# One core, two networks in a row: the RW lanes of the mixer stage split into an edge thread and a body thread

## The reference, cut to what matters

```
zr = z_rw + (token_shift(z_rw) - z_rw) * rw_mu
r, kr, vr, xw, xa, xg = split(zr)                       # 16 heads of 64
decay = exp(-exp(-softplus(-(rw_w0 + tanh(xw) @ rw_w2)) - 0.5))
a  = sigmoid(rw_a0 + xa @ rw_a2);  g = sigmoid(xg) @ rw_g2
kk = kr * rw_kk;  kk = kk / max(norm(kk), 1e-12)
kr = kr * (1 + (a - 1) * rw_ka)
S_t = S_{t-1} (diag(w_t) - kk_t^T (a_t*kk_t)) + v_t^T k_t ;  y_t = S_t r_t     # per head, 64 x 64
y  = groupnorm(y) * rw_ln_g + rw_ln_b + sum(r*kr*rw_rk) * vr;   y = y * g
out = concat([o_gla, y]) @ w_out
```

## Time and profile before

| | us |
|---|---|
| median of 3 runs | 3964.98 (3961.74 to 3965.10) |
| the profiled execution | 3966.74 |
| its span (first to last instruction) | 3965.0 |
| TensorE busy | 3651.3 (92%) |
| VectorE busy | 2321.6 (59%) |
| ScalarE busy | 1791.0 (45%) |
| mean granted TensorE clock | 0.946 |

### The profile page before, as it was taken

The page is one execution under the profiler, slowest core; times in us unless marked ns, Lnnn a source line. Parts: engine busy times, 40 slices in busy tenths (PEclk is TensorE's granted clock), DMA queues, the critical chain, the costliest instruction groups (busy, mean ns, idle before and its releaser), DMA issues.

```text
span 3965.0 us, 77817 instructions
## 1 busy us (share of the span) xinstructions
PE 3651.3 (92%) x29460; PEld 3538.5 (89%) x29460; DVE 2321.6 (59%) x3394; ACT 1791.0 (45%) x2463; POOL 217.2 (5%) x306
## 2 busy tenths in 40 slices
PE   7976989999999898888878899999998999999998
PEld 6976989999999898777767899999997999999998
DVE  3687566656665634454444566656656756856555
ACT  3322455544444533333333455544444546475443
POOL 1371100000000000000000200000000000000000
PEclk9988999999999998788888899999999999999999
DMA  4533556566656543111111466666664665556774
GB/s 132 152 112 96 152 145 181 170 177 189 175 167 176 160 128 91 43 43 38 43 38 49 123 184 182 177 198 183 181 175 130 165 167 146 152 138 177 196 193 143
DMA packets 1103441, 561.56 MB, mean 142 GB/s; under 512 B 23011, under 2 KB 1101429, under 8 KB 1102981
## 3 DMA queue, kind: packets, MB, share of 16 engines
q1 hardware_dynamic: 1100672, 553.98, 49.7%
q10 hardware_dynamic: 1957, 2.83, 0.2%
q0 software_dynamic: 624, 2.13, 0.2%
HBM read 556.77 MB, written 2.10 MB: 141 GB/s over the span
## 4 chain that ended last, share of the span: by engine, by line
issue 90%; POOLq 5%; PE 3%; DVE 1%; ACTq 0%; POOL 0%; ACT 0%; DMA 0%; DVEq 0%
POOLq L727 2%; POOLq L725 2%; POOLq L507 1%; PE ps L346 1%; PE ps L347 1%; PE ps L348 1%; PE ps L521 0%; ACTq L2130 0%; DVE arena L552 0%; POOLq L723 0%; PE ps L2154 0%; POOLq L2301 0%; DVE ps L548 0%; POOLq L2304 0%; POOLq L2224 0%
## 5 line engine op out<-in xcount | busy, mean ns | idle before, releaser
L314 DVE TENSOR_TENSOR w_lo<-raw,w_hi 128x1024 fp32r<-128x1024 f32 (+1 forms) x1136 | 1333.1, 1185 | 882.0 <-ACT w_hi L308 876.7
L308 ACT ACTIVATE w_hi<-raw 128x1024 fp32r<-128x1024 f32 (+1 forms) x1136 | 1144.0, 1016 | 696.5 <-PE ps L348 445.2
L346 PE MATMUL ps<-x_hi,w_hi 128*128 128x272 f32 (+1 forms) x3712 | 1076.7, 290 | 79.7 <-DVE w_lo L314 44.0
L347 PE MATMUL ps<-x_lo,w_hi 128*128 128x272 f32 (+1 forms) x3712 | 1072.4, 289 | 0.0
L348 PE MATMUL ps<-x_hi,w_lo 128*128 128x272 f32 (+1 forms) x3712 | 1072.0, 289 | 0.0
L430 PE MATMUL ps<-x_hi,w_hi 128*128 128x256 f32 (+4 forms) x2944 | 890.1, 302 | 56.3 <-DVE x_lo L546 16.2
L431 PE MATMUL ps<-x_lo,w_hi 128*128 128x256 f32 (+4 forms) x2944 | 849.0, 288 | 0.0
L432 PE MATMUL ps<-x_hi,w_lo 128*128 128x256 f32 (+4 forms) x2944 | 847.8, 288 | 0.0
L346 PEld LDWEIGHTS ps<-x_hi,w_hi 128*128 128x128 f32 x3712 | 715.7, 193 | 86.8 <-DVE w_lo L314 48.3
L347 PEld LDWEIGHTS ps<-x_lo,w_hi 128*128 128x128 f32 x3712 | 716.0, 193 | 0.0
L348 PEld LDWEIGHTS ps<-x_hi,w_lo 128*128 128x128 f32 x3712 | 715.3, 193 | 0.0
(11 more groups left out here) (442 smaller groups left out, 3396.5 us busy)
## 6 DMA issues: line engine op xcount, KB each, us to landing
raw<-ffn_w_up SPq DMA_DIRECT2D x352, 512.0 KB, 4.7
raw<-w_in SPq DMA_DIRECT2D x232, 512.0 KB, 3.8
raw<-cd_w_in SPq DMA_DIRECT2D x100, 512.0 KB, 3.8
raw<-ffn_w_down SPq DMA_DIRECT2D x128, 384.0 KB, 3.4
raw<-ab_w_in SPq DMA_DIRECT2D x80, 512.0 KB, 4.5
raw<-ffn_w_down SPq DMA_DIRECT2D x128, 320.0 KB, 3.3
raw<-w_out SPq DMA_DIRECT2D x48, 512.0 KB, 4.0
raw<-ab_w_out SPq DMA_DIRECT2D x32, 512.0 KB, 4.0
```

The source lines that it names most:

```text
L308: nc.scalar.activation(w_hi[:, j % SLOTS, 0:kt], raw[:, j % RING, 0:kt], ACT.Copy).then_inc(rounded, 1)
L314: nc.vector.tensor_tensor(w_lo[:, j % SLOTS, 0:kt], raw[:, j % RING, 0:kt], w_hi[:, j % SLOTS, 0:kt].bitcast(F32), ALU.subtract).then_inc( ...
L346: nc.tensor.matmul(acc, w_hi[:, j % SLOTS, k, 0:w], mh, start=first, stop=False)
L347: nc.tensor.matmul(acc, w_hi[:, j % SLOTS, k, 0:w], ml, start=False, stop=False)
```

## The change

The work of a lane is cut in two threads per engine, with semaphores of their own. `edge_*` does the front of a pair and its 16 meta tokens, in the lane's banks B + 1 and B + 2. `body_*` does the two tiles of 128 tokens (in all three banks), the chunk states and the end (in bank B alone). So the edge of a lane's next pair is issued beside the last states and the end of the pair before. Its gates wait for `fe2` of that pair, no longer for its end; its first wide tile waits for both the edge's `fe0` and the old pair's end.

```
+    def rw_start(p):
+        return MID_PARTS["pairs"] + 6 * p + 4.1
...
+    EDGE_AT, EDGE_END = timed((("keys", 1.0), ("gates", 1.9), ("rates", 2.0), ("norm", 0.6), ("cum", 3.4), ("decays", 0.1), ("bonus", 2.5), ("ready", 2.9),
...
+            ("x", 1.6), ("m", 1.5), ("p2", 1.0), ("p2_", 0.9), ("p4", 1.9), ("p4_", 1.1), ("p8", 1.3), ("p8_", 0.7), ("y8", 0.5), ("y8_", 0.7),
+            ("z1", 0.8), ("z1_", 0.7), ("w", 0.5), ("t32", 0.7), ("gh", 0.5), ("gh_", 0.6), ("fe", 2.6), ("fe_", 2.7))], BODY_END)
```

Four of the seven chunk states move into the second tile's steps. A state product is put behind the products of p4, p8, y8 and w, its addition behind theirs; only s6, s7 and s8 stay in a row:

```
+                mm = heads_times(B + 2, 0, L.p4, of(L.y), n, n)
+                if tt == 2:
+                    mm = next_state(2, B + 2, 2 * P)
+                done(mm)
...
+                mm = nc.vector.tensor_tensor(L.y, L.y, two_of(B + 2, 0, n), add)
+                if tt == 2:
+                    mm = next_state(2, B + 2, 2 * P)
+                done(mm)
```

Within a step, the mask that p2 needs (`q1`) is taken straight from PSUM ahead of the others, and p2 waits for it alone; `y` is waited for one step later. One ScalarE copy of 512 columns takes the place of two or three of 256 and 128 at p2 and p4:

```
-                done(nc.vector.tensor_tensor(L.p1[0:n, :, 0:n], res(2), over(low16), mult))
+                done(nc.vector.tensor_tensor(L.q1, ps[:, B:B + 2, 0:n], over(up16, n), mult))
...
-                vector(f"m{tt}")
+                vector(f"q1{tt}")
...
+                done(nc.scalar.activation(L.pq2, ps[:, B + 2].rearrange("p (a b) -> p a b", a=4), ACT.Copy))
```

```
+            for hh in range(2):
+                rows = slice(64 * hh, 64 * hh + 64)
+                if hh:
+                    pe.wait_ge(L.row_sem, 4 * q + 4)
+                for c in range(1, 9):
+                    state = L.state0[q % 2] if c == 1 else L.state[:, c - 1]
+                    first = P + (c - 1) * RW_CHUNK
+                    mm = nc.tensor.matmul(ps[rows, B, first:first + RW_CHUNK], state[rows], L.f[rows, c - 1], start=True, stop=True)
```

More of the change, by code:

```diff
@@ L204, in build @@
     low21, _ = place("low21", [P, P])
-    eye2, _ = place("eye2", [P, RW_N])
     seg, _ = place("seg", [P, T])
@@ L990, in build @@
     rws_s, RWS_S = sem("rws_scalar"), order("low")
-    def tile_stages(*stages):
-        return [f"{st}{tt}" for tt in range(3) for st in stages if tt or st not in ("z1", "w", "t32", "t16")]
-    RW_V = order("keys", "norm", "cum", "bonus", "ready", *tile_stages("p1", "m", "q2", "q4", "y4", "y8", "z1", "t32", "fe"),
-                 *[f"s{c}" for c in range(2, 9)], "y", "centred", "end")
-    RW_S = order("rates", "norm", "decays", *tile_stages("tok", "p2", "p4", "p8", "t16", "gh", "add"), "squared", "rstd")
@@ L1009, in build, with body_stages @@
-    RW_AT = {name: RW_LEN * x / at_ for name, x in RW_AT.items()}
-    def rw_start(p):
-        return MID_PARTS["pairs"] + 6 * (p + 1) + 0.1
-    def rw_vector(dve, lane_n):
-        L, mult, add, sub = lanes[lane_n], ALU.mult, ALU.add, ALU.subtract
-        B = L.b
-        yield GLA_END + 5.5
-        dve.drain()
-        nc.vector.memset(L.trans, 0.0)
-        dve.drain()
+    BODY_TILES = (1, 2)
+    def body_stages(*stages):
+        return [f"{st}{tt}" for tt in BODY_TILES for st in stages]
@@ new lines, in build @@
+    EDGE_V = order("keys", "norm", "cum", "bonus", "ready", "q10", "y0", "q40", "y40", "y80", "fe0")
+    EDGE_S = order("rates", "norm", "decays", "tok0", "p20", "p40", "p80", "gin0", "gh0", "add0")
+    EDGE_T = order("gates", "bonus", "x0", "p20", "p40", "p80", "y80", "gh0", "fe0")
+    BODY_V = order(*body_stages("p1", "q1", "y", "q4", "y4", "y8", "z1", "t32", "fe"), "s6", "s7", "s8", "y", "centred", "end")
+    BODY_S = order(*body_stages("tok", "p2", "p4", "p8", "gin", "t16", "gh", "add"), "squared", "log", "rstd")
@@ new lines, in build, with timed @@
+    BODY_T = order(*body_stages("x", "p2", "p4", "p8", "y8", "z1", "w", "gh", "fe"), "s6", "s7", "s8", "out", "sums", "squares", "gate")
+    RW_LEN = 2 * 6
+    def timed(stages, first=0.0):
+        at, now = {}, first
+        for name, step in stages:
+            at[name] = now
+            now += step
+        return at, now
+    EDGE_AT, EDGE_END = timed((("keys", 1.0), ("gates", 1.9), ("rates", 2.0), ("norm", 0.6), ("cum", 3.4), ("decays", 0.1), ("bonus", 2.5), ("ready", 2.9),
+                               ("x0", 1.3), ("m0", 1.1), ("p20", 0.3), ("p20_", 0.6), ("p40", 0.8), ("p40_", 0.7), ("p80", 0.5), ("p80_", 0.6),
+                               ("y80", 0.2), ("y80_", 0.5), ("gh0", 0.4), ("gh0_", 0.6), ("fe0", 0.5), ("fe0_", 1.2)))
@@ new lines, in build, with over, two_of, edge_vector @@
+    BODY_AT.update(some)
+    EDGE_AT, BODY_AT = ({name: RW_LEN * x / BODY_END for name, x in at_.items()} for at_ in (EDGE_AT, BODY_AT))
+    TAIL_AT = RW_LEN * TAIL_END / BODY_END
+    def rw_start(p):
+        return MID_PARTS["pairs"] + 6 * p + 4.1
+    def over(mask, n):
+        return mask[0:n, 0:n].unsqueeze(1).to_broadcast([n, 2, n])
+    def two_of(b, first, n):
+        return ps[0:n, b, first:first + 2 * n].rearrange("p (a b) -> p a b", a=2)
+    def edge_vector(dve, lane_n):
+        L, mult, add, sub, n = lanes[lane_n], ALU.mult, ALU.add, ALU.subtract, META
+        X, Y = L.b + 1, L.b + 2
@@ new lines, in edge_tensor, with body_tensor, of, value @@
+            done(mm)
+    def body_tensor(pe, lane_n):
+        L, n = lanes[lane_n], P
+        B = L.b
+        for q in range(PAIRS_RW // 2):
+            p = 2 * q + lane_n
+            done = lambda ins: ins.then_inc(L.bt, 1)
+            vector = lambda name: pe.wait_ge(L.bv, q * len(BODY_V) + BODY_V[name])
+            scalar = lambda name: pe.wait_ge(L.bs, q * len(BODY_S) + BODY_S[name])
+            at = lambda name: rw_start(p) + BODY_AT[name]
+            def of(buf, first=0):
+                return lambda hh: buf[:, first + hh]
+            def value(hh):
+                return L.v_tok[:, 64 * hh:64 * hh + 64]
+            def next_state(c, b, first):
+                before = L.state0[q % 2] if c == 1 else L.state[:, c - 1]
+                return nc.tensor.matmul(ps[:, b, first:first + RW_N], L.trans[:, c - 1], before, start=True, stop=True)
+            for tt in BODY_TILES:
+                t0 = TILES[tt][0]
+                cols_ = slice(t0, t0 + n)
```

584 lines of the change are left out of this document (342 added, 242 removed).

## The result

The changed kernel takes 3843.89 us (median of 4 runs, 3824.6 to 3850.05) where the kernel before takes 3965.04 us beside it: ratio 0.9676, 95% interval 0.9637 to 0.9715. The forecast was 3920 us in a range of 3870 to 3990 us. The direction is right; the gain is 121 us where 45 were forecast.

The account below looks back on a forecast made before the run. TensorE bounds the kernel, losing time to waits and low clock in the RW pairs. Waits -3.6, work -0.7 and clock -1.8 make -6.1 us a pair, -49 over eight, +4 at the end: 3920 us, range 3870 to 3990.

Parts of the forecast that it names:

- Waits that come: TensorE's waits per pair in the new order: 11.7 us, 10.5 as the trace counts, against 14.1 before; term -3.6 us.
- A: TensorE's wait at the squares of the old pair, behind ScalarE's rounding, loads, Ln and Exp: 3.2 us.
- C: TensorE's wait at edge 1's scores, behind VectorE's last operations of the old pair and the ready block: 3.3 us.
- D: TensorE's wait at edge 1's p2, whose ScalarE copies wait for masks queued on VectorE: 1.8 us.
- E: TensorE's wait at y8 of body 0, behind a `w_lo` and a tap: 1.5 us.
- B: TensorE's wait at tile 2 of body 0, behind ScalarE's queue and VectorE's transitions: 1.0 us.
- Own work: TensorE's own work per pair, with state and output products merged into other groups or runs: 0.7 us less, between 0 and 1.5.
- Clock: TensorE's low clock per pair: price falls from 4.6 to 2.8 us as five long waits become three, -1.8 us.
- The output jobs: Start of the output jobs: the 7.0 us wait stays, plus 4 us once for copies amid the last pair's ready block.
- Warm all the way: Rival: TensorE's clock stays up between the fewer waits, a cycle is 65.3 us, 3898 us in all; chance 0.15.
- The waits only move: Rival: A to E add up to the old 14.1 us, clock stays at 0.82, 3959 us; chance 0.15.
- The slower case: Rival: the edge's chain on ScalarE comes later and lengthens A, B and C; 4000 us, 4035 at worst; chance 0.17.

Follow-up runs that it names:

- e11: The changed kernel run again unchanged, beside the version with grouped functions and a later end on the same chip: 3842.78 us, ratio 0.9684 to the kernel before.
- e6: The kernel before with only its position table changed to the new distances, without threads or overlap: 3902 us, ratio 0.9840 to the kernel before.
- e4: The changed kernel with the norm's square made 17 times on ScalarE, so TensorE waits long at one place: 3935 us, ratio 0.9912 to the kernel before.

## Why the prediction was wrong

In the whole stretch, 116.4 us: waits go from 115 to 59.5 us (-55.5), the low clock from 235.5 to 79.1 us (at 0.4, -63), the rest is +2. By the second trace of the changed kernel (e11) it is 131 us: -59.5, -71, and the rest 0. So the clock gives somewhat more than the waits; the split hangs on the 0.4.

*Waits that come.* Right in place, a little high in size. A 3.2 against 2.6, C 3.3 against 2.4, D 1.8 against 2.15, E 1.5 against 0.8, B 1.0 against nothing; in all 8.1 against the 10.5 forecast and 13.4 in five cycles before. Per cycle -5.3 against -3.6.

*Own work.* Forecast -0.7 a pair. The rest is 54.0 and 54.1 before and 53.3 and 53.1 after: -0.9. Right, as far as single traces tell.

*Clock: the step that failed,* a term that was mis-sized. "Mean cycle less warm cycle, 74.2 - 69.6 = 4.6 us, is the price of the low clock per pair." Two errors are in it. The mean of the keys holds the first cycle, in which one lane runs alone and there is less to do; full cycles take 77.5 us, so by the same subtraction the price would be 7.9. And the warm cycle is one of 0.98, so the price must come from the clock's share of the full ones: 25.3 us x 0.4 = 10 us a pair. The trace of the kernel before has it in the products themselves:

```profile
1783.04 0.43 PE L431 MATMUL ps<-x_lo,w_hi 128*128 128x272 f32 x1
1783.27 0.43 PE L432 MATMUL ps<-x_hi,w_lo 128*128 128x272 f32 x1
```

Behind the z1 wait a stream product comes every 0.23 us, where the earlier trace rows have 0.13 us. The forecast read the lengths (0.43 against 0.29), which show less of it. Of the 10 us 7.7 went, not 1.8. "In proportion 4.6 becomes 2.8" failed too: long waits fell from five to three a cycle at most, the low clock to a quarter. In the stretch the term is -63 us against 8 x -1.8 = -14; that is 48 of the 76 us missed.

The Trainium skill states that slow is the resting state of this clock (TensorE: Matmul & The Clock Gate, "The HAM clock gate"). The trace of e4 agrees: the clock falls 1.9 us into the wait of 10.4 us and comes back 8.6 us after TensorE has started again.

*Eight pairs alike* was the second, smaller miss. The waits of the first pairs and of the run-out fell more than those of a cycle: 19.4 to 9.7 us up to the first sums and 28.8 to 9.4 us behind the sixth, -29 together, where three pairs at -3.6 make -11. With the cycles' -26.5 against -18 the waits are 27 us of the miss.

*The output jobs.* +4 us forecast; their wait went from 7.0 to 2.9, which is part of the waits above. Clock 48, waits 27 and these 4, less 7 for the rest (+1.7 us in the stretch where -5.6 was forecast), make 72 of the 76 us; the remainder lies between the stretch and the medians.

*The new distances* had no price of their own in the forecast, which went through the new order as a whole, and alone they give half of the gain (e6).

*The rivals.* Warm all the way (3898 us) came nearest in mechanism, with the same wrong subtraction as its price. The waits only move: they fell by half. The slower case rested on ScalarE's chain growing by 3 us; e4 has far more than that at A, 10.4 us, and is still faster than the kernel before.

The Trainium skill gives a switch of tables a load of 1283 ns and a drain of some 1380 ns (ScalarE: Activation LUTs, "What ACT_TABLE_LOAD costs"). The trace of after agrees with the load, 1.28 us, and not with the drain: L1237's load starts 0.06 us behind Ln, ends at 1907.00, and Exp starts at 1907.01.

*What the signs said.* Keys 60 us apart and a clock of 0.93 between the first and the last keys go beyond the "66 to 70" and "0.85 or more"; in the full cycles the idle is 2.6 us before the squares and 2.4 us before the scores, in four of five, where "about 3" was written, and none before p2 of the wide tiles and the z1 users.

## What to carry to other kernels

Price the clock apart from the waits: take the time at 1.2 GHz from the granted clock of a window in which all lanes are full, leave out what lies inside waits, and charge about 0.4 of the remainder; do not subtract one good cycle from a mean. The 0.4 is of this kernel; two filled waits of your own give yours. A useless product in a wait of an otherwise idle TensorE is a cheap test of that price, and where nothing better is at hand a gain: 37 us here. Before steps are split or moved, try the distances between them alone.
